# Constant matmuls into an unused PSUM bank while TensorE waits, in a two-layer decoder trunk

## What is computed

```python
h = rms_norm(x, norm_mix_g[l]); proj = h @ w_in[l]
o_r = rwkv7_mixer(token_shift(p_r, shift_mu[l]), ...)      # 8 heads of 64
o_m = mla_mixer(p_m, positions, ...)                       # 4 heads, causal attention
o_g = gmlp_mixer(p_g, ...)                                 # spatial gating in chunks of 128
x = x + jnp.concatenate([o_r, o_m, o_g], axis=-1) @ w_out[l]
h = rms_norm(x, norm_mem_g[l])
x = x + memory_cross_attention(h, mem_k, mem_v, mem_w_q[l], mem_q_g[l], mem_w_o[l])
h = rms_norm(x, norm_ffn_g[l])
x = x + hierarchical_moe(h, ...)                           # 32 experts of 512, top 2 of one group
```

## Time and profile before

| | |
|---|---|
| median of 3 runs | 2416.16 us (2408.09 to 2421.2) |
| the profiled execution | 2416.59 us |
| its span, first to last instruction | 2414.8 us |
| mean granted TensorE clock over the span | 0.929 |
| busy in the span: PE, DVE, ACT, POOL | 2127.0, 731.0, 391.0, 33.5 us |
| bytes moved by DMA | 481.36 MB, 199 GB/s over the span |

### The profile page before, as it was taken

How to read it: one execution, slowest core, us unless ns; L and a number is a source line. 1 busy time by engine, 2 the same in 40 slices (tenths; PEclk the granted TensorE clock), 3 DMA queues, 4 the chain that set the end, 5 groups by cost and what they waited for, 6 DMA issues and landing times. The chain is left out here.

```text
span 2414.8 us, 25286 instructions
## 1 busy us (share of the span) xinstructions
PE 2127.0 (88%) x10248; PEld 1198.0 (50%) x10248; DVE 731.0 (30%) x1337; ACT 391.0 (16%) x734; POOL 33.5 (1%) x80
## 2 busy tenths in 40 slices
PE   3999989699779999999579998978987999999964
PEld 2445888454454444443234488845445444444322
DVE  2244653442441111111234464434244111111103
ACT  2112110341310000000022211034131000000000
POOL 1000000000000000000100000000000000000001
PEclk8999998799889999999879999989988999999996
DMA  3400000220139999999750000021004899999983
GB/s 129 168 0 1 1 1 1 111 105 0 40 135 411 428 429 428 427 429 427 288 210 1 0 1 1 1 111 66 39 0 174 362 428 428 429 429 427 429 331 143
DMA packets 47357, 481.36 MB, mean 199 GB/s; under 512 B 7136, under 2 KB 7904, under 8 KB 19488
## 3 DMA queue, kind: packets, MB, share of 16 engines
q1 hardware_dynamic: 44960, 471.65, 46.7%
q0 software_dynamic: 2304, 8.39, 1.0%
HBM read 461.14 MB, written 18.87 MB: 199 GB/s over the span
## 5 line engine op out<-in xcount | busy, mean ns | idle before, releaser
L1696 PE MATMUL bank<-ring,hT 128*64 128x512 f32 x2048 | 456.7, 594 | 23.4 <-DMA ring<-in_we 20.1
L1696 PEld LDWEIGHTS bank<-ring,hT 128*64 128x64 f32 x2048 | 145.9, 137 | 322.7 <-issue 281.6
L684 PE MATMUL bank<-hT,ring 128*128 128x512 f32 (+1 forms) x608 | 269.5, 604 | 1.9 <-DVE hT L408 1.9
L1703 PE MATMUL bank<-ring,arena 128*64 128x512 f32 x1040 | 244.7, 613 | 16.8 <-DVE arena L1875 15.9
L1689 PE MATMUL bank<-arena 128*128 128x256 f32 x1024 | 251.4, 391 | 6.7 <-DVE arena L1716 6.7
L1689 PEld LDWEIGHTS bank<-arena 128*128 128x128 f32 x1024 | 188.9, 193 | 75.9 <-issue 47.1
L1875 DVE TENSOR_TENSOR arena<-arena,bank 128x256 f32<-128x256 f32 x64 | 27.0, 421 | 571.3 <-ACT arena L1817 570.8
L684 PEld LDWEIGHTS bank<-hT,ring 128*128 128x128 f32 (+1 forms) x608 | 116.2, 193 | 151.2 <-issue 148.9
L1815 ACT ACTIVATE arena<-bank 128x512 f32<-128x512 f32 x64 | 38.2, 597 | 799.8 <-PE bank L1696 799.8
L1703 PEld LDWEIGHTS bank<-ring,arena 128*64 128x64 f32 x1040 | 72.8, 140 | 152.1 <-issue 150.9
L1402 PE MATMUL bank<-hT,ring 128*128 128x512 f32 x256 | 110.3, 593 | 2.9 <-PEq L96 2.9
(11 more groups left out here) (399 smaller groups left out, 2192.2 us busy)
## 6 DMA issues: line engine op xcount, KB each, us to landing
ring<-in_we SPq DMA_DIRECT2D x195, 2048.0 KB, 21.2
expert_rows<-arena SPq DMA_DIRECT2D x128, 128.0 KB, 18.5
ring<-in_w_in SPq DMA_DIRECT2D x6, 2048.0 KB, 16.7
ring<-in_w_out SPq DMA_DIRECT2D x4, 2048.0 KB, 9.8
ring<-in_wm SPq DMA_DIRECT2D x2, 2048.0 KB, 16.3
ring<-in_w_in SPq DMA_DIRECT2D x2, 1920.0 KB, 7.8
ring<-in_w_in SPq DMA_DIRECT2D x2, 1664.0 KB, 24.4
ring<-in_w_in SPq DMA_DIRECT2D x2, 1152.0 KB, 26.8
```

The lines of the kernel that those rows point to most:

```text
L684: last = nc.tensor.matmul(B[n % 4][0:w, :], ins_units[unit][:, k, u0:u0 + w], hT[:, k, :], start=k == 0, stop=k == KD - 1)
L1696: last = nc.tensor.matmul(bank[CAP * j:CAP * j + CAP, :], x[:, k, :], up_w(u, j, k), start=k == 0, stop=k == KD - 1)
L1703: last = nc.tensor.matmul(bank[CAP * half:CAP * half + CAP, :], hid[u][:, m, :], down_w(u, m, half), start=m == 0, stop=m == HM - 1)
```

## The change

A helper `keep_busy(bank, n, w)` issues `n` matmul calls of `w` columns. They multiply the identity by `mask4` into a bank that holds nothing at that moment; no semaphore is touched and nothing reads the result. Calls of it are put into TensorE's list at eighteen places: ahead of waits in the setup, the norms, latent attention, cross-attention, routing, the start of the experts, and the combine. The counts are fixed numbers. P is 128.

```diff
+        def keep_busy(bank, n, w):
+            for _ in range(n):
+                nc.tensor.matmul(bank[:, 0:w], ident[:, :], mask4[:, 0:w // P, :], start=True, stop=True)
...
@@ setup, behind the sums of the memory tokens' squares
+                keep_busy(B[6], 18, P)
                 eng.wait_ge(s_mh, KD)
@@ start of a layer
+                    keep_busy(B[6], 7, 4 * P)
                     norm_mean(eng, 0, nrm_acc)
+                    keep_busy(B[6], 3, P)
                     norm_spread(eng, 0)
+                    keep_busy(B[6], 3, P)
@@ latent attention
                     eng.wait_ge(s_upc, 8)
+                    keep_busy(B[7], 14, 4 * P)
                     for z in range(8):
@@ behind the output projection
+                    keep_busy(B[6], 6, P)
                     norm_mean(eng, 1, nrm_acc)
+                    keep_busy(B[6], 4, P)
                     norm_spread(eng, 1)
+                    keep_busy(B[6], 3, P)
@@ cross-attention
                     last.then_inc(s_q2, 1)
+                    keep_busy(B[6], 2, P)
                     eng.wait_ge(s_q5, 1)
...
+                    keep_busy(B[6], 8, P)
                     eng.wait_ge(s_q4, 2)
...
                         last.then_inc(s_xs, 1)
+                        if h == 1:
+                            keep_busy(B[6], 6, P)
+                        if h == 2:
+                            keep_busy(B[7], 6, P)
                         if h >= 2:
                             flip_x(eng, h - 2)
...
+                    keep_busy(B[6], 6, P)
                     norm_mean(eng, 2, nrm_acc)
+                    keep_busy(B[6], 3, P)
@@ routing
                     norm_spread(eng, 2)
+                    keep_busy(B[6], 3, P)
...
+                    keep_busy(B[1], 3, 4 * P)
                     eng.wait_ge(s_rt2, 1)
@@ start of the experts
+                    keep_busy(B[7], 8, P)
                     eng.wait_ge(s_sel, 1)
@@ combine
+                    keep_busy(B[7], 10, 4 * P)
                     for i in range(NT):
                         eng.wait_ge(s_cb, i + 1)
```

## The result

The change takes 2390.28 us (median of 4 runs, 2383.09 to 2397.2), the kernel before, run beside it, 2418.52 (4 runs, 2408.09 to 2421.2): a ratio of 0.9867, interval 0.9841 to 0.9894, so 28 us faster where 25 were forecast. The interval is clear of no change, and the difference is 1.3%. The profiled execution of the change is the slowest of its four, 2397.2 us, its span 2395.1. The mean granted clock went from 0.929 to 0.955. The time at the 0.50 level, added up over the trace, fell from 344.9 to 218.4 us. TensorE was busier than before, 2191.8 instead of 2127.0 us, and the kernel is shorter.

The account below looks back on a forecast made before the run. DMA bounds the experts; elsewhere others wait for TensorE, slowed by its half clock. Terms 1.2 + 6.2 + 1.0 + 8.8 + 6.4 + 6.4 = 30.0 us, less 5 for failures: 25 off 2416.6, 2392 us; range 2376 to 2408.

Parts of the forecast that it names:

- The price of a call: On TensorE, a wide call costs 0.89 us at full clock and 1.8 at half, a narrow one 0.24 and 0.49.
- Start of a layer: Seven wide calls raise the clock before the mean, ending up to 0.7 or 1.1 us late: -6.2 us for both layers.
- Setup: 18 narrow calls fill 4.4 us of a 6.17 us pause; half of a possible 2.4 us is taken: -1.2 us.
- Latent attention: Fourteen wide calls ahead of the flips; 2.8 us could come back per layer, 0.5 taken: -1.0 us.
- The norms: Behind the two output projections, narrow calls around the mean give 4.4 us per layer: -8.8 us.
- Cross-attention: From the third head on, 4.7 us less per layer, minus 1.5 for six uncovered calls: 3.2 per layer, -6.4 us.
- Routing and the experts' start: Rank sums 2.6, half the gather's gain 1.2, less 0.6 for eight narrow calls: 3.2 per layer, -6.4 us.
- Combine: Ten wide calls end up to 1.7 us late, the transposes win 1.0; put at 0.
- The allowance of 5 us for stretches that fail: Of six stretches of norms and cross-attention, one or two lose the clock at some 3 us each: 5 us in all.
- that the calls do not raise the clock: Rival: identity multiplications do not count as busy, calls run at half speed and overrun: 2477 us, chance 0.05.
- That short pauses are not the cause: Rival: one-column matmuls and 32-column sums may cost the clock; norms and cross-attention stay slow: 2404 to 2410 us, chance 0.17.
- Everything is held: Rival: half of all slow work in the touched stretches returns, 40 us: 2377 us, chance 0.12 for 2382 and below.

Follow-up runs that it names:

- the trimmed one: The change without six calls behind the third head's scores, eight at the experts' start and ten in the combine: 2390.06 us, ratio 0.9862.
- the run above: The change with three calls ahead of the barrier in the norm behind cross-attention replaced by two behind it: 2383.44 us, one run.
- the one with other data: The change with added calls multiplying the memory's values by its keys, except the setup's 18: 2388.21 us, ratio 0.9876.
- the kernel with the short pauses alone: The change keeping only the calls in the norms behind the two output projections and in cross-attention: 2409.82 us, ratio 0.9947.
- the one with more places: The change plus calls in RWKV, group norm, latent attention's start, between rank sums; third head's six removed, experts' start's eight made four: 2363.53 us, 0.9759.
- the kernel with the longer calls: The one with more places, with more calls in setup, latent attention and norms, six of latent attention's moved behind its first copies: 2362.33 us, 0.9755.

## Why the prediction was right, point by point

- **The price of a call** was right: the 36 instructions in the setup's pause and the 28 in latent attention run at 0.12 and 0.44 us each, and the raising of the clock at a layer's start took 5.36 us of slow work in layer 0, between the 3 and 6 that were allowed.
- **Start of a layer** gave 5.2 and 5.1 us in the two profiles instead of 6.2. From the mean on it gave 7.0 and 7.1. The calls end late, as foreseen, but in layer 1 by 1.4 and 1.3 us instead of 0.8: TensorE comes to them 1.4 us behind ScalarE's first instruction there (1202.31 against 1200.93), against 0.1 in layer 0. The forecast let them begin together. In layer 0 they ended 0.7 us late in the second profile and in time in the first.
- **Setup**, taken as half because 1.8 us stay empty, was right for that reason: 2.15 us stayed. Of eight profiles with 18 calls there (transposes in one) five have the 32 instructions of L332 in 7.17 us instead of 9.60; in three (the second profile of the change, the one with transposes, the trimmed one) the clock fell 1.1 to 1.4 us behind their start and they took 8.86. So a single run gets 2.4 or 0.7 us, and 1.2 is a fair guess between them and no measured value.
- **Latent attention** was under-sized: 3.7 us instead of 1.0. The clock was held through 1.96 us (1.82 with transposes) in all eight profiles with these calls, and ScalarE's copies did not stand in the way.
- **The norms** were over-sized by 1.3 us: 7.5 instead of 8.8. The first was right (4.5 against 4.6). In the second the forecast overlooked that the calls behind the mean stand ahead of a barrier; the run above gives 0.75 us a layer back.
- **Cross-attention** was about right, 6.0 against 6.4, with the six uncovered calls at 1.4 instead of 1.5 us.
- **Routing and the experts' start** gave 7.3 instead of 6.4, by another split than foreseen: the rank sums won 1.7 us up to their end, but the clock fell at their end and the eight calls ran slow, 3.51 us instead of 2.0, so up to the start of the gather the step is +0.3. The clock was up again when the gather began. It gave 2.6 us a layer, and the first L1703 (L1725) behind it 1.4, on which the forecast had not counted.
- **Combine** at nothing was right. Ten calls ended 0.9 us behind VectorE in layer 0 and its add (L1996) covered that. The 2.4 us that the step to L2028 shows are these 0.9 and 1.5 from the last expert's L1725, which ran slow (5.35 us for 16 instructions instead of 3.65). From there to ScalarE's first instruction of layer 1 the change lost 1.3 us (1.0 in its second profile), the trimmed kernel, with no call in the combine, 1.7, and the one with other data won 0.7. The ten calls do not order these numbers; where the clock falls in the last turns of the experts differs from profile to profile, and that it decides was not tested by itself.
- **The allowance of 5 us for stretches that fail** was not needed: none of the norms or of cross-attention failed. Of the 30.0 us of the sum the touched parts gave 31.8 and 30.5, and what took the place of the allowance are the 2.7 us around the combine and, in the first profile, 9.3 us of chance in RWKV. The mechanism was right; that the total came out within 2 us of 2392 owes something to luck, since latent attention and the allowance, both held too gloomily, stand against the norms, the late calls and the combine.
- The rivals: that the calls do not raise the clock is refuted (5.36 us, then 1.00), also for transposes. That short pauses are not the cause is refuted by the kernel with the short pauses alone. "Everything is held" promised 40 us; the touched parts gave 30 to 32. The calls still run slow at the experts' start and at a layer's start; that a part of the slow work stood beside VectorE and ScalarE is argued and was not measured by itself.
- Two numbers of the text: the 21.6 us gross of its six stretches are half of the slow work of both layers (21.5 by the earlier trace rows), while its own terms, 2.6 + 2.4 + 4.7 a layer, give 19.4. No number of the forecast hangs on it.

Still open: the norm behind cross-attention kept its clock in all seven profiles that have the six calls of the third head and calls in this norm. It lost it at its spreading in the trimmed kernel and in the one with more places, in both layers of each, which have the same calls around that norm but not the six, some 30 us earlier. The kernel with the longer calls has not got the six either and kept it, with nine calls ahead of the mean and five behind it; it took 1.0 us less there, not 1.5. Why the absence of the six matters was not settled. Nor was it tried what decides how long the clock stays down in RWKV.

## What to carry to other kernels

Where TensorE waits some 2 us again and again and runs at half clock behind the waits, read the stretches behind the waits: half of the slow work there that is on the chain is the most that filling the wait can give back. Fill the wait with instructions of 128 or 512 columns into a free bank, not of one, count them so that they end just short of it, and never place them ahead of a barrier that others wait for; the clock's mean alone says little, since twice the calls had the better clock and were 28 us slower than no calls at all. Before a stretch that the edit does not touch is blamed on it, take a second profile of both kernels.

## What the runs showed of the hardware

- One-column instructions occupied TensorE as long as narrow ones (0.12 us) and did not keep the clock up: with them in all eighteen places the norm behind the output projection fell to 0.50 as before, for 10.24 us instead of 6.8, and the kernel took 1.0083 of the time.
- Transposes and constants held the clock as dense data did (0.958, 0.955 and 0.963 in the profiled executions, 2386.61, 2390.28 and 2388.21 us), and either raised it from 0.50 by themselves at a layer's start, behind 5.86 and 5.36 us of work.
- The same pause can cost the clock or not: behind 2.15 us ahead of the setup's projection (2.24 with transposes) it fell in three profiles of eight, behind 1.96 us ahead of latent attention's flips in none of eight.
- A pause of 1.58 us among small matmuls (64 and 128 columns, in RWKV) is where the clock falls in every profile without calls there; the same fall lasted 7, 10 or 27 us from one execution to the next. By the busy time in it, 24.6 us against 5.9, the longest costs some 9 us more than the shortest (an estimate), where 19 runs of this kernel span 18 us. In the two kernels with calls in that pause it did not come.
